# A PEER layer's value table: all rows gathered, or half of its columns by one dense product

## The reference, cut to what matters

```
q = (hb @ w_query)                                   # 8 heads x 2 halves x 128
s = q . sub_keys                                     # 8 x 2 x 128 scores a token
top_s, top_i = top_k(s, 16)
best_s, best_j = top_k(all sums of one score of each half, 16)
idx = i * 128 + j                                    # i, j in 0..127
g = softmax(best_s)
a = gelu(u[idx] . hb)
out = sum over heads and k of (g * a) * v[idx]       # v: 16384 x 2048
```

## Time and profile before

| | |
|---|---|
| three runs | 3405.6, 3405.66, 3398.89 us; median 3405.6 |
| span of the profiled execution | 3402.5 us |
| last sublayer's gathers, first to last landing | about 2143 to 3392 us |
| PE, DVE, ACT, POOL busy | 74%, 52%, 32%, 69% of the span |
| moved by DMA | 868 MB, of it 537 MB by the gathers |

### The profile page before, as it was taken

How to read it: one execution, slowest core, us unless ns; L and a number is a source line. 1 busy time by engine, 2 the same in 40 slices (tenths; PEclk the granted TensorE clock), 3 DMA queues, 4 the chain that set the end, 5 groups by cost and what they waited for, 6 DMA issues and landing times.

```text
span 3402.5 us, 42238 instructions
## 1 busy us (share of the span) xinstructions
PE 2507.2 (74%) x15833; PEld 1974.7 (58%) x15833; DVE 1781.8 (52%) x2456; ACT 1081.7 (32%) x2108; POOL 2364.1 (69%) x1677
## 2 busy tenths in 40 slices
PE   7999996989999999989999899108503730571077
PEld 5777885779988998889988679103201310230032
DVE  4375656242200223220412446997797879778954
ACT  6444424464444444454546554000000100000000
POOL 7400316859999999987866579886687578568853
PEclk9999997999999999999999999559856965796589
DMA  5684300546655665555544346999999999999998
GB/s 180 206 237 145 105 3 26 185 123 183 185 191 187 183 183 185 187 153 161 161 131 125 117 164 206 396 427 427 427 428 427 427 427 427 428 426 427 427 427 344
DMA packets 241376, 868.10 MB, mean 255 GB/s; under 512 B 18940, under 2 KB 21484, under 8 KB 174886
## 3 DMA queue, kind: packets, MB, share of 16 engines
q0 software_dynamic: 73776, 536.97, 37.5%
q1 hardware_dynamic: 163414, 316.11, 30.6%
q10 hardware_dynamic: 4016, 12.75, 1.3%
HBM read 860.24 MB, written 2.10 MB: 253 GB/s over the span
## 4 chain that ended last, share of the span: by engine, by line
PE 50%; POOL 19%; DMA 11%; DVE 7%; issue 4%; ACT 1%; DVEq 0%; ACTq 0%; POOLq 0%; SPq 0%
PE acc L2022 20%; PE acc L2032 19%; DMA zone<-in_peer_v,zone 10%; POOL lasting L736 10%; POOL zone L736 9%; PE acc L2028 3%; PE acc L2160 3%; PE acc L2586 2%; POOL w_lo L616 1%; DVE lasting L1962 1%; DMA lasting<-in_peer_u,zone 1%; PE acc L2475 1%; DVE zone L1568 0%; PE acc L2069 0%; DVE x_lo L1697 0%
## 5 line engine op out<-in xcount | busy, mean ns | idle before, releaser
L616 POOL TENSOR_TENSOR w_lo<-lasting,w_hi 128x512 fp32r<-128x512 f32 x1024 | 1372.4, 1359 | 276.0 <-ACT w_hi L785 257.3
L785 ACT ACTIVATE w_hi<-lasting 128x512 fp32r<-128x512 f32 (+1 forms) x1184 | 741.3, 631 | 903.6 <-PE acc L2022 457.0
L2586 PE MATMUL acc<-zone,lasting 128*128 128x512 f32 x512 | 256.3, 655 | 694.3 <-ACT lasting L1297 643.4
L2586 PEld LDWEIGHTS acc<-zone,lasting 128*128 128x128 f32 x512 | 105.2, 210 | 841.6 <-ACT lasting L1297 505.2
L2032 PE MATMUL acc<-x_hi,w_hi 128*128 128x256 f32 (+1 forms) x1856 | 305.5, 286 | 11.5 <-DVE x_lo L1697 4.3
L736 POOL DMA_INDIRECT zone<-in_peer_v,zone x128 | 192.2, 1502 | 165.6 <-DVE lasting L1962 73.6
L1932 DVE CUSTOM_DVE_ANT_0 zone<-zone 128x2048 f32<-128x2048 f32 x128 | 293.4, 2292 | 21.9 <-DMA zone<-in_peer_u,zone 7.1
L1932 DVE CUSTOM_DVE_ANT_0 zone<-lasting,zone 128x2048 f32<-128x2048 f32 x128 | 293.5, 2293 | 21.0 <-DMA lasting<-in_peer_u,zone 8.6
L2032 PE MATMUL acc<-x_lo,w_hi 128*128 128x256 f32 (+1 forms) x1856 | 298.6, 283 | 0.0
L2032 PE MATMUL acc<-x_hi,w_lo 128*128 128x256 f32 (+1 forms) x1856 | 298.3, 283 | 0.0
L2586 PE MATMUL acc<-lasting 128*128 128x512 f32 x512 | 247.8, 635 | 64.9 <-DMA zone<-in_peer_v,zone 38.2
(11 more groups left out here) (419 smaller groups left out, 3951.7 us busy)
## 6 DMA issues: line engine op xcount, KB each, us to landing
lasting<-in_w_in SPq DMA_DIRECT2D x200, 512.0 KB, 3.7
lasting<-in_w_up SPq DMA_DIRECT2D x128, 512.0 KB, 3.8
lasting<-in_w_down SPq DMA_DIRECT2D x128, 512.0 KB, 3.6
lasting<-in_w_mix_out SPq DMA_DIRECT2D x32, 512.0 KB, 3.6
lasting<-in_w_out SPq DMA_DIRECT2D x32, 512.0 KB, 3.6
lasting<-in_peer_w_query SPq DMA_DIRECT2D x32, 512.0 KB, 3.7
lasting<-in_w_kv_cross SPq DMA_DIRECT2D x16, 512.0 KB, 3.7
lasting<-in_w_q_cross SPq DMA_DIRECT2D x8, 512.0 KB, 3.7
```

Source lines behind the costliest of these rows:

```text
L616: pool.tensor_tensor(w_lo[:, k, 0:width], ring[:, slot, s % SLOT_SLABS, 0:width], w_hi[:, k, 0:width].bitcast(FP32), ALU.subtract).then_in ...
L785: act.activation(w_hi[:, s % PARTS, 0:width], ring[:, slot, s % SLOT_SLABS, 0:width], ACT.Copy).then_inc(hi_ready, 1)
L2586: last = pe.matmul(bank(4 * t + c), diag[:, n // 2, k], rows_buf[2 * n + k][:, c * CHUNK:(c + 1) * CHUNK], start=hx % 2 == 0 and i == 0 an ...
```

## The change

The second half of v's columns (1024 to 2047) is still gathered, now as half rows of 4 KB, 256 gathers of 0.5 MB. The first half (columns 0 to 1023) is not gathered. Instead a dense matrix C, 256 tokens x 16384 experts, is built in SBUF (`dense`, 128 KB in each partition), and the product C x v[:, 0:1024] is made with all of v's first half streamed once: 128 tiles of 128 rows x 1024 columns, 0.5 MB each.

- **C**: expert i * 128 + j of token s. For each token a one-hot matrix of i (128 experts x 128) and one of j, scaled by the coefficient, are made, and their product is C[s]. Tile 0's one-hots are made by ACT (Abs, Relu, Copy with scale), beside the dot products of tile 1; tile 1's by DVE (`one_hots`: eight tensor_scalar of 128x128 for 4 tokens, 32 groups), after the last dot product. PE multiplies, ACT copies the bank to `dense`.
- **Order**: POOL gathers all 256 u rows first, and beside u rows 80 to 212 the first 96 half rows of v (`V_AFTER`), which PE weighs with diagonals. All eight `choose` now lie among tile 0's dot products or before (`CHOOSE_AFTER`). The second tile has only 8 row buffers for u, since C takes the place of others; v's half rows have 4 buffers of 0.5 MB.
- **Then** a loop over the 128 tiles of v: SP loads a tile (4 buffers); ACT rounds it to float32r (128x1024) and copies C's columns (128x256, a stride of 512 bytes); DVE subtracts for the low part of columns 0 to 767 and of C; POOL subtracts columns 768 to 1023; PE makes 12 float32r products of 128x512; DVE weighs one or two of the other 160 half rows (128x1024), which POOL gathers in the same loop.

The core of the diff:

```diff
+        U_SPOTS = [...19 places...]
+        FIRST_TILE, SECOND_TILE = (5, 7, 8, 13, 4, 6, 0, 1, 9, 10, 11, 12, 14, 15), (5, 7, 8, 13, 4, 16, 17, 18)
+        V_EARLY = 96
+        V_AFTER = {80 + k: k for k in range(64)} | {150 + 2 * k: 64 + k for k in range(V_EARLY - 64)}
+        CHOOSE_AFTER = {40: (0, 2), 64: (0, 3), 88: (1, 0), 104: (1, 1), 118: (1, 2), 126: (1, 3)}
+        COEFS_AFTER = {66: 0, 129: 1, 220: 2, 255: 3}
+        BY_DVE = 768
...
# SP
+            for i in range(N_KEYS):
+                if i == 2:
+                    sp.wait_ge(s_dense, GROUPS)
+                if i >= 4:
+                    sp.wait_ge(s_vlo_dve, i - 3)
+                    sp.wait_ge(lo_ready, V_SLAB + i - 3)
+                sp.dma_start(v_raw[:, i % 4], A["peer_v_2"][0][i * P:(i + 1) * P, 0:HALF_D]).then_inc(tile_full[i % 4], 16)
...
# POOL
+            def gather_v(q):
+                if q >= V_EARLY + 4:
+                    pool.wait_ge(s_wdve, q - 4 - V_EARLY + 1)
+                elif q >= 4:
+                    pool.wait_ge(s_wpe, q - 4 + 1)
...
+            for q in range(7, U_SLOTS):
+                gather_u(q)
+                if q in V_AFTER:
+                    gather_v(V_AFTER[q])
+            done = V_EARLY
+            for i in range(N_KEYS):
+                while done < min(U_SLOTS, V_EARLY + 4 + (i * (U_SLOTS - V_EARLY - 4)) // (N_KEYS - 4)):
+                    gather_v(done)
+                    done += 1
+                pool.wait_ge(hi_ready, V_SLAB + i + 1)
+                pool.tensor_tensor(v_lo[:, i % 2, BY_DVE:], v_raw[:, i % 4, BY_DVE:], v_hi[:, i % 2, BY_DVE:].bitcast(FP32),
+                                   ALU.subtract).then_inc(lo_ready, 1)
...
# ACT
+            act.wait_ge(s_denseR, GROUPS)
+            for i in range(N_KEYS):
+                act.wait_ge(tile_full[i % 4], 16 * (TURNS + i // 4 + 1))
+                if i >= 2:
+                    act.wait_ge(slab_used, PARTS + V_SLAB + i - 1)
+                act.activation(v_hi[:, i % 2], v_raw[:, i % 4], ACT.Copy)
+                act.activation(dense_now[:, 0, i % 2], dense[:, :, i], ACT.Copy).then_inc(hi_ready, 1)
...
# DVE
+            for g in range(GROUPS // TILES, GROUPS):
+                one_hots(g)
+            done = V_EARLY
+            for i in range(N_KEYS):
+                dve.wait_ge(hi_ready, V_SLAB + i + 1)
+                TT(v_lo[:, i % 2, 0:BY_DVE], v_raw[:, i % 4, 0:BY_DVE], v_hi[:, i % 2, 0:BY_DVE].bitcast(FP32), ALU.subtract)
+                TT(dense_now[:, 1, i % 2], dense[:, :, i], dense_now[:, 0, i % 2].bitcast(FP32), ALU.subtract).then_inc(s_vlo_dve, 1)
+                while done < V_EARLY + ((i + 1) * (U_SLOTS - V_EARLY)) // N_KEYS:
+                    weigh_half_row(done)
+                    done += 1
...
# PE
+            def v_tiles(i, first=False, final=False):
+                for k in range(2):
+                    pe.wait_ge(s_vlo_dve, i * 2 + k + 1)
+                    pe.wait_ge(lo_ready, V_SLAB + i * 2 + k + 1)
+                    for n, (cp, vp) in enumerate(((0, v_hi), (1, v_hi), (0, v_lo))):
+                        for t in range(TILES):
+                            for c in range(2):
+                                last = pe.matmul(bank(2 * t + c), dense_now[:, cp, k, t * P:(t + 1) * P], vp[:, k, c * CHUNK:(c + 1) * CHUNK], ...)
+                    last.then_inc(slab_used, 1)
```

More of the change, by code:

```diff
@@ L404, in build @@
         following = dict(zip(list(G)[:-1], list(G)[1:]))
+        TURNS = sum(g.turns * g.bodies for g in G.values())
         tile_full = [sem(f"tile_full{i}") for i in range(SLOTS)]
@@ L1283, in exp_gates, with gelu_dots @@
                 act.activation(part, part, ACT.Exp).then_inc(s_be, 1)
-            exp_gates(0)
-            for hx in range(2 * TILES):
+            def gelu_dots(hx):
                 act.wait_ge(s_dot, hx + 1)
@@ new lines, in _ @@
+            act.wait_ge(s_coefs, 1)
+            for q in range(48):
+                diagonal(q)
+            exp_gates(2)
+            exp_gates(3)
+            gelu_dots(1)
+            for q in range(48, 64):
+                diagonal(q)
+            act.wait_ge(s_keysT, 1)
+            act.activation(keysT.rearrange("p k s -> p (k s)"), bank(6), ACT.Copy).then_inc(s_keysR, 1)
+            act.wait_ge(s_coefs, 2)
+            act.wait_ge(s_keysR, 1)
+            read_coefs(0)
+            for g in range(GROUPS // TILES):
+                one_hots(g)
+                if g:
+                    read_dense(g - 1)
+                if 64 + g < V_EARLY:
+                    diagonal(64 + g)
@@ new lines, in turn_coefs, with dense_group @@
+            def turn_coefs(t):
+                pe.wait_ge(s_coefs, 2 * t + 2)
+                if t:
+                    pe.wait_ge(s_denseR, GROUPS // TILES)
+                pe.transpose(bank(7)[:, 0:P], coef[:, t], ident).then_inc(s_coefT, 1)
+            def dense_group(g):
+                pe.wait_ge(s_hot, g + 1)
+                if g >= 2:
+                    pe.wait_ge(s_denseR, g - 1)
+                for n in range(4):
+                    last = pe.matmul(bank(6 + g % 2)[:, n * P:(n + 1) * P], hot_of(g, 1)[:, n], hot_of(g, 0)[:, n], start=True, stop=True)
+                last.then_inc(s_dense, 1)
@@ new lines, in _ @@
+            for q in range(64):
+                weigh_half_row(q)
+            pe.wait_ge(s_keys, 1)
+            for k in range(2 * TILES):
+                last = pe.transpose(bank(6)[:, k * P:(k + 1) * P], split_keys[:, k], ident)
+            last.then_inc(s_keysT, 1)
+            turn_coefs(0)
+            for g in range(GROUPS // TILES):
+                dense_group(g)
+                if 64 + g < V_EARLY:
+                    weigh_half_row(64 + g)
+            turn_coefs(1)
+            for g in range(GROUPS // TILES, GROUPS):
+                dense_group(g)
@@ L2593 @@
+            v_tiles(0, first=True)
+            loop(pe, N_KEYS // 2 - 1, v_tiles, 1)
+            v_tiles(N_KEYS // 2 - 1, final=True)
 def kernel(**inputs):
```

314 lines of the change are left out of this document (193 added, 121 removed).

## The result

The changed kernel takes 3650.76 us (median of 4 runs, 3645.02 to 3655.46) against 3402.24 for the kernel before (3397.17 to 3405.66): ratio 1.0728 [1.0712, 1.0744], slower by 248 us. The direction was forecast, the size was not: 3513 was predicted, 138 us less, and the range ended at 3630.

A forecast was written before the change was run, and what follows sets the result against it. The stage was bound by bytes; in the new loop DVE and POOL's subtraction would add at the SBUF port. Loop start 3011 + 493 + 5.5 at the end = 3510 us of span, 3.1 more for the median: 3513, range 3395 to 3630.

The forecast's parts named there:

- Part 1: All u rows and the first 96 half rows: last dot done at 2925 us, bounds 2890 and 2955.
- Part 2: Tile 1's half of the matrix, uncovered: 256 tensor_scalar on DVE at 0.30 us, 77 us, bounds 56 and 95.
- Part 3: Loop over 128 tiles of v with 160 half rows: 3.85 us a tile, 493 us, bounds 410 and 550.
- the second coupling, the ring: Loop: POOL's gathers wait for DVE's weighing, PE for POOL's subtraction; 3.2 to 4.3 us a tile, middle 3.76.
- the long form of the ring: Loop: slow gathers (3.0), POOL waiting for a weighing, DVE for a subtraction: 13.0 us in three tiles, 4.3 a tile.
- The port: Loop: DVE's work and POOL's subtraction add, 3.1 + 0.735 = 3.85 us a tile; rival that it does not bind, chance 0.20.
- The gathers: On POOL, a gather takes 0.95 us alone and 2.11 beside DVE's dots; with issue, 1.25 and 2.42 in the loop.
- about 20 us less: Loop, if DVE does not hold up gathers, as the page infers: POOL's share of the ring stays at 1.56.
- PE's clock: Rival, chance 0.05: in the loop at 1.2 GHz, 12 products take 5.6 us, 714 us in all, total 3734.
- Landing: Rival, chance 0.13: in the loop, four half-row buffers set 3.0 to 4.3 us a tile, total to 3570.
- bytes or PE bound the loop: Rival, chance 0.12, the side of faster: 2.79 us a tile, 357 us in the loop, total 3377.
- the sum's 2.75: Loop's bytes for one tile and 1.25 half rows at the earlier rate: 1.22 + 1.25 x 1.22 = 2.75 us.

The follow-up runs named there:

- e2_pace: The changed kernel with POOL's gather pace in the loop made equal to DVE's, 160/128 of a half row a tile instead of 156/124: 3567.0 us.
- e1_sub_first: The changed kernel with POOL's subtraction of a tile placed before that tile's gathers, pace kept: 3501.8 us.
- e3_dve_all: The changed kernel with DVE subtracting all 1024 columns of v's tile and POOL only gathering: 3463.2 us.
- e6_both: The changed kernel with both POOL's subtraction before the gathers and the equal pace of 160/128: 3487.7 us.
- e10_ring_only: Probe: e9_three without the loop's 160 half rows, neither gathered nor weighed, so the output lacks them: 3373.0 us.
- e15_free: Probe: e11_unweighed with gathers no longer held to the tiles' pace, four always under way: 3418.2 us.
- e9_three: e3_dve_all with every fifth loop half row weighed by PE, four buffers of `v_hi` and three for C's columns: 3460.7 us.
- e14_all_one_queue: The complete e9_three with v's tiles issued by POOL on the gathers' queue instead of by SP: 3459.7 us.
- e11_unweighed: Probe: e10_ring_only with the loop's 160 half rows gathered at the tiles' pace but none weighed: 3462.6 us.

## Why the prediction was wrong, step by step

- **Part 1** was right: the last dot ends at 2939 where 2925 was said (bounds 2890 to 2955), 14 us late.
- **Part 2** was a little high: 59 us for 256 tensor_scalar, one every 0.23 us, where 0.30 and 77 us were taken. The DMA gap came (0.23 at 92 GB/s). ACT takes the first tile at 3001.7; by the forecast, 3011 less the 6 us of filling, it was 3005. The two misses nearly cancel.
- **Part 3 is the step that failed.** 3.85 us a tile were forecast and 4.98 measured: 128 x 1.13 = 145 us, more than the whole miss of 138. The term that was wrong is the second coupling, the ring, in two places. First, "The middle is 3.76; I take the port's 3.85": the long form of the ring (slow gathers, POOL waiting for a weighing) gave 4.3, and e2_pace, in which POOL's wait is always as the prediction described it, measures 4.31. The long form was not a bound but the value, 0.46 x 128 = 59 us. That 4.3 and 4.31 agree so closely is partly luck: in e2_pace ACT's two operations have means of 1.06 and 0.65 us where 1.43 was taken for both, and the clock is 0.94. Second, "POOL may issue the gathers of tile i only when DVE has weighed the half rows of tile i-1": so it is only with equal paces. The diff's 156/124 against 160/128 makes it tile i's own weighing ever more often; 84 us, by e2_pace. 59 and 84 are 143, and 149 is what the order alone gives back. Where POOL waits for the tile's own weighing, a turn of the ring carries two tiles and not three: 12.6 us for two late in the changed kernel, 3 x 4.31 = 12.9 for three in e2_pace, against 13.0 in the long form. The parts of the 12.6 are others, though: PE's 12 products take 5.5 us of it at the low clock, where 2.79 was taken, and the gather 1.64 where 3.0 was.
- **The port** was taken rightly in kind and too large. In e1_sub_first a tile takes 3.80 us, against 3.1 + 0.735 = 3.85; without POOL's subtraction beside it (e3_dve_all) it takes 3.53. But DVE's operations are not held for all of POOL's 0.735: their means rise by 0.27 us (128x256), 0.14 (128x768, 1.10 against 0.96 where nothing holds it) and 1.25 x 0.06 (weighing, 1.34 against 1.28), 0.49 a tile, an estimate. So the 3.85 is near 3.80 in part by luck, and e6_both, with equal pace, measures 3.71. In the changed kernel the port was a term beside a longer ring and not the bound. Single sizes were off: ACT's 256 columns with a stride took 0.65 us and not 0.38, DVE's 0.57 to 0.61 at best and not 0.43.
- **The gathers** are held as the earlier trace rows had it: in the loop 1.61 us where DVE weighs (L807, 3510.84: 1.64) and 0.96 where it waits. The page "SBUF — State Buffer" of the Trainium skill, section "Who interferes with whom", infers that a DVE operation with two SBUF inputs does not hold up descriptor generation; for these gathers the traces differ. But such a gather also reads its row numbers from SBUF (`half_rows_no`, the `lasting` on the right of L807's rows), and no run parts that reading from the generation of descriptors. The "about 20 us less" that the prediction gives for the page's case does not follow from its own sum, whose loop goes by the port's 3.85, without a gather in it.
- **PE's clock** had 0.05 as a rival of its own at 3734. It fell in part (0.91, then 0.79), as an effect of the ring, at a price of some 27 us or more. PE's 2.79 us a tile at full clock was exact (e10_ring_only).
- **Landing** of half rows was not the bound: before its weighings DVE stood 3.0 us in the whole loop. A half row lands 8.3 us after its issue with four always under way (the median in e15_free); the prediction took 7.5 to 8.7, and by its own sum that is 3.0 to 4.0 a tile. The page "DMA: Bandwidth & Descriptors" of the Trainium skill, section "Anatomy of one DMA — SWDGE (gpsimd) path", gives an estimate of 3.2 us for it. No run here shows a half row so fast. Landing of the tiles, which no rival named, is a part of the bound from e9_three on.
- **Bytes.** The rival "bytes or PE bound the loop" at 2.79 a tile is what e10_ring_only reaches, but only without the half rows. With them the loop's transfers never moved at the 424 GB/s of the earlier trace rows; in no complete kernel were they over 344 (e14_all_one_queue). At that rate, 3.4 us a tile, the total is near 3002 + 439 + 10 = 3451, slower than before even with order and ring mended: that is the deeper flaw of the sum's 2.75, though 3.85 hid it. The rate is what four small buffers for each stream gave, and not a limit of the queues (e15_free).

No complete version beats the kernel before (3402 us). The best, e14_all_one_queue, e9_three and e3_dve_all, lie within 4 us of each other at 3460 to 3463. Two things stay against all of them: 60 us of part 2, in which the DMA queues stand nearly still, and the loop's rate. Whether more buffers would help the complete kernel was not tried. By e15_free, more gathers under way would not make the tiles faster; and e15_free itself, with nothing weighed, still takes 3418.

## What to carry to other kernels

Where an engine's in-order list holds both a prefetch that waits for a free buffer and work that another engine waits for, put the work first: the order alone was worth 149 us of 3651 here. When two loops are paced by fractions, compare the fractions over the whole loop, not at its start: 1.258 against 1.25 cost 84 us. And when a stage bound by deep-queued gathers is traded for one with four small buffers for each stream, don't take the old stage's GB/s along, and when the total rate rises, look which stream has gained: in e15_free it was not the one that the loop waited for.

## What the hardware showed that was not expected

- Both DMA streams together moved 340 GB/s at a DMA share of 0.94 (e11_unweighed) and 398 at 1.02 with four gathers always under way (e15_free); the gathers alone, deep in the queue, 424 at 1.00. v's tiles alone showed a share of 0.62 at 188 GB/s (e10_ring_only), about 300 GB/s for each unit of share. The share is no straight measure of what is left.
- With 256 columns read at a stride of 512 bytes DVE's subtraction took 0.57 to 0.61 us, against 0.43 estimated for a dense one, and ACT's copy 0.65, against 0.38 in the earlier trace rows. That row reads a bank and not SBUF, and no run has the dense form, so the stride's share is not shown.
- PE's granted clock fell to 0.79 with PE busy 68% in the last stretch, in gaps of 4 us, and was 1.00 in e1_sub_first with PE busy 82% (196 of 240 us). Eight products took 3.78 us at the lower level and 2.13 at the higher.
